# Backward sweep of a state-space scan: two products a chunk made by ScalarE, in sixteen pieces each, in place of VectorE

## The chip, the cores and the metric

The kernel runs on one core of a Trainium2 chip. A core has five engines with an instruction queue each: TensorE (matmuls, PE in the profile, with its weight loads as PEld), VectorE (DVE), ScalarE (ACT), GpSimd (POOL) and SyncE (SP). Each engine works through its queue strictly in order; semaphores tie the queues together. The metric is the device time of one launch in microseconds, as a median over runs.

## The reference, cut to what matters

The program computes two transformer-like blocks, one after the other, over 1024 tokens of width 1024. The change lies in the second block, in the backward half of a two-directional scan over chunks of 128 tokens, with 16 heads of 64 channels and a state of 128:

```python
def ssd_chunked(xs, dt, a, bm, cm, h0):
    ...
    st = jnp.einsum('bcsgn,bcsgr,bcsgrp->bcgrpn', bc, jnp.exp(acs[:, :, -1:] - acs), xdt)
    def step(s, inp):
        dec, add = inp
        return s * dec[..., None, None] + add, s
    ...
    y_off = jnp.einsum('bctgn,bcgrpn,bctgr->bctgrp', cc, s_in, jnp.exp(acs))
    return (y_diag + y_off).reshape(b, l, h, p), s_final

def bidir_ssd(xs, dt, a_log, bm, cm, h0_f, h0_b):
    ...
    y_f, s_f = ssd_chunked(xs, dt[:, :, 0], a[0], bm, cm, h0_f)
    y_b, s_b = ssd_chunked(rev(xs), rev(dt[:, :, 1]), a[1], rev(bm), rev(cm), h0_b)
    return y_f + rev(y_b), s_f, s_b
```

For a chunk, the sweep reads the state as it stands (`y_off`), then decays the state by a factor per head and adds what the chunk brings (`st`, a product of the chunk's keys with its values, the values weighed by a factor for each token and head). To the chunk's output comes also each token's own value times a factor for that token and head (the diagonal and the skip term `d_skip * xs`). Two of these are plain multiplications of a chunk's values, 128 tokens by 16 heads by 64 channels, by a number for each token and head: the own share, and the weighed values. In the kernel tokens lie on the partitions, so for one head such a number is one column of 128, and the head's values are 128x64.

In the same stretch the box means over the 16 by 64 token grid (`pool_mixer`) are made, and projections of the layer's input.

## The kernel before

`phase5` holds the scan. Its first loop is the backward sweep: eight passes, i from 0 to 7, over the chunks c = 7 - i. After it comes the forward sweep, and after that the rest of the block. All that follows is laid out engine by engine in written order; semaphores are the only ties.

One pass i, engine by engine, in queue order:

- **TensorE**: `off(0, c)`, four matmuls of the state with the chunk (L2473), once the state of pass i-1 is there; then `add_state`, four matmuls with the weighed values `xw` (L2459), once `xw_ready` says they are there; then one or two projection tiles of 48 matmuls each (`gemm`; lines L230, L232, L234). Pass 0 has one tile, passes 1, 2, 3 and 6 have two (u and z), passes 4, 5 and 7 one. The u tile goes to a pair of PSUM banks that must have been read out since the last u tile.
- **VectorE**: own share into `y_even` (L2747, after the previous `y_even` has landed in memory, `y_back`); the state's share of the output (L2749, after `off`); their sum (L2751, which signals `y_ready`); the state's decay and update (`sum_state`, L2699 and L2700, which frees the way for the next `off`); the next pass's weighed values `xw` (`weigh`, L2696); then `pool_tile(i)` (L2726 several times, L2732, L2733), the box means of the u tile, which waits until ScalarE has copied that tile out of PSUM (`pair_free`). It is 10 instructions in passes 0 and 1, 8 in 2 and 3, 6 in 4 and 5, 4 in 6 and 7. The last signals `pooled`.
- **ScalarE**: waits for `y_ready` and issues the store of `y_even` (L2617); copies the u tile out of PSUM (L2621) once it is made; in passes 0, 1, 2, 3 and 6 a Silu of a z tile and its store (L2608, L2610); waits for `pooled` and issues the store of the box means (L2593); after passes 1, 3 and 5 issues a load of the divisors (`load_area`, L2589). After pass 0 it also makes 16 scaled copies of 128x128 for the forward sweep (`make_moving(0, j)`, L2600), which nobody needs before that sweep.
- **GpSimd**: splits each weight tile into a high and a low part (L221, L223), two tiles ahead.
- **SyncE**: streams the weight tiles in.

Of the kernel before, what the change touches and what calls it, by code (L numbers as in the profile page):

```python
# [11 lines left out]
ACT = mybir.ActivationFunctionType  # L12
# [5 lines left out]
NC = SEQ // P  # L18
# [26 lines left out]
CC = CTX // P  # L45
TOK2 = CTX + SEQ
SSM_HEADS = 16
HDIM = 64
# [89 lines left out]
def bc(ap, dim, n):  # L138

    ap = ap.unsqueeze(dim)  # L140
    shape = list(ap.shape)
    shape[dim] = n
    return ap.broadcast_to(shape)
# [895 lines left out]
def signals(nc, ctx, stage, names):  # L1039

    return {n: ctx.enter_context(nc.semaphore(f"{stage}_{n}")) for n in names.split()}
# [1318 lines left out]
def phase5(nc, k, d, v):  # L2360
# [4 lines left out]
    with ExitStack() as ctx:  # L2365
        def sb(n, shape, dt=F32):
            return ctx.enter_context(nc.sbuf_tensor(n, shape, dt))

        state, y_even, xw = (sb(n, [P, SEQ]) for n in ("state5", "y5", "xw5"))
# [18 lines left out]
        ctx_values = [xw, y_even, big[:, 2, :], xw]  # L2388
        stage = k.ada_w
        s = signals(nc, ctx, "p5", "chain xw_ready moving_ready d_done chosen e_ready w_ready cb_done cb_ready off_done fore_ready "  # L2390
                                   "st_done state_ready diag_done y_ready y_back y_out0 y_out1 u_in0 u_in1 u_in2 u_in3 z_out d_out "
                                   "dhi dlo x_done x_free0 x_free1 cleared area_in pooled")
        x_free = [s["x_free0"], s["x_free1"]]
        y_out, u_in = [s["y_out0"], s["y_out1"]], [s[f"u_in{t}"] for t in range(SPLIT_EARLY)]
# [5 lines left out]
        BWD_JOBS = 2  # L2400
        after = v.consts[:, SC_FORE:SC_FORE + P].bitcast(I32)

        back = 2 * CC
        fwd = back + BWD_JOBS * NC

        def u_tile(i):
            return XBC_END + i + sum(c < i for c in Z_CHUNKS)
# [8 lines left out]
        def heads(ap):  # L2416
            return ap.rearrange("p (h n) -> p h n", h=SSM_HEADS)

        def values(c):
            return heads(v.tok[:, c, VAL:VAL + D_MODEL])  # L2420

        def per_head(buf, c, r, n=HDIM):

            return bc(buf[:, c, SSM_HEADS * r:SSM_HEADS * (r + 1)], 2, n)
# [162 lines left out]
        def _(act):  # L2587
            def load_area(g):
                act.dma_start(big[:, 3, :], d.pool_area[g, :, :]).then_inc(s["area_in"], 16)  # L2589

            def rows_out(i, t):
                act.wait_ge(s["pooled"], i + 1)
                act.dma_start(d.u_scr[t, :, :].rearrange("p (r c) -> p r c", r=ROWS), pooled).then_inc(s["d_out"], 16)  # L2593

            def make_moving(i, j):

                if i:
                    act.wait_ge(s["d_done"], QUADS * (i - 1) + j + 1)
                for h in range(j * QUAD, (j + 1) * QUAD):
                    ins = act.activation(moving[:, h, :], v.x_rows[:, i * P:(i + 1) * P], ACT.Copy,  # L2600
                                         scale=v.consts[:, SC_HEAD + h:SC_HEAD + h + 1])
                ins.then_inc(s["moving_ready"], 1)

            def z_out(i, q):
                n = z_tile(i)
                act.wait_ge(k.tile_done, n + 1)
                act.wait_ge(s["z_out"], 16 * i)
                act.activation(stage[:, :], pair[q], ACT.Silu).then_inc(k.pair_free[n % 2], 1)  # L2608
                act.wait_ge(k.pair_free[n % 2], n // 2 + 1)
                act.dma_start(d.z_scr[i, :, :], stage[:, :]).then_inc(s["z_out"], 16)  # L2610

            load_area(KT // 2 - 1)
            act.wait_ge(s["cleared"], 2)
            for i in range(NC):
                c, t = NC - 1 - i, KT - 1 - i
                act.wait_ge(s["y_ready"], i + 1)
                act.dma_start(d.y_tok[c, :, :], y_even[:, :]).then_inc(s["y_back"], 16)  # L2617
                n = u_tile(i)
                act.wait_ge(k.tile_done, n + 1)
                act.wait_ge(s["pooled"], i)  # L2620
                act.activation(u_mid, pair[n % 2].rearrange("p (r c) -> p r c", r=ROWS), ACT.Copy)\  # L2621
                   .then_inc(k.pair_free[n % 2], 1)
                if i in Z_CHUNKS:
                    z_out(Z_CHUNKS.index(i), 1)
                rows_out(i, t)
                if t % 2 == 0 and t:
                    load_area(t // 2 - 1)
                if i == 0:
                    for j in range(QUADS):
                        make_moving(0, j)  # L2630
# [59 lines left out]
        def _(dve):  # L2690
            ch = Chain(dve, s["chain"])
            tt = dve.tensor_tensor

            def weigh(c, r, out=xw[:, :]):

                tt(heads(out), values(c), per_head(v.w_st, c, r), ALU.mult).then_inc(s["xw_ready"], 1)  # L2696

            def sum_state(c, r, q):
                ch.link(tt(heads(state[:, :]), heads(state[:, :]), per_head(v.e_tot, c, r), ALU.mult))  # L2699
                tt(state[:, :], state[:, :], Xf[q], ALU.add).then_inc(x_free[q], 1)  # L2700
# [42 lines left out]
            weigh(NC - 1, 1)  # L2743
            for i in range(NC):
                c = NC - 1 - i
                dve.wait_ge(s["y_back"], 16 * i)
                ch.link(tt(heads(y_even[:, :]), values(c), bc(v.own[:, c, :], 2, HDIM), ALU.mult))  # L2747
                dve.wait_ge(s["x_done"], back + BWD_JOBS * i + 1)
                tt(heads(back_tmp), heads(Xf[0]), per_head(v.e_acs, c, 1), ALU.mult).then_inc(x_free[0], 1)  # L2749
                dve.wait_ge(x_free[0], back // 2 + i + 1)  # L2750
                tt(y_even[:, :], y_even[:, :], back_tmp, ALU.add).then_inc(s["y_ready"], 1)  # L2751
                if c:
                    dve.wait_ge(s["x_done"], back + BWD_JOBS * i + 2)
                    sum_state(c, 1, 1)
                    if c > 1:
                        weigh(c - 1, 1)
                    else:
                        weigh(0, 0)
                else:
                    dve.tensor_copy(state[:, :].rearrange("p (a n) -> p a n", a=4), state_f).then_inc(s["state_ready"], 1)  # L2760
                pool_tile(i)
# [464 lines left out]
```

## Time and profile before

| | us |
|---|---|
| Median of 3 runs | 2821.09 (2818.49 to 2828.03) |
| The profiled execution's own time | 2826.55 |
| Its span | 2824.8 |
| TensorE busy | 2659.1 (94%) |
| VectorE busy | 1638.1 (58%) |
| ScalarE busy | 609.5 (22%) |
| GpSimd busy | 995.2 (35%) |

The span is what the profiler recorded of one execution; its own time lies 1.75 us above the span. TensorE's share is near full over the whole program, so a stretch matters to the end as far as it makes TensorE stand still or run at the lower clock. The backward sweep lies at about 1544 to 1708 us of the span.

### The profile page before, as it was taken

How to read it: one execution, taken by the hardware profiler on the slowest of the kernel's cores; microseconds unless marked ns; L12 is line 12 of the kernel's file. 1: busy time of each engine (PE TensorE's matmuls, PEld its weight loads, DVE VectorE, ACT ScalarE, POOL GpSimd, SP SyncE). 2: the span in 40 equal slices, each digit the busy share in tenths (PEclk: the TensorE clock that was granted, in tenths of full speed). 3: DMA queues.
4: the chain of work that ended last, by engine and by line, in shares of the span. 5: the costliest groups of instructions: out<-in, count | busy, mean ns of one | idle time of the engine just before them, and what ended most of it. 6: DMA issues, size and time to landing. Idle time of an engine off the chain costs nothing. (4 is left out here: it accounts for less than half of the span.)

```text
span 2824.8 us, 32083 instructions
## 1 busy us (share of the span) xinstructions
PE 2659.1 (94%) x12350; PEld 2143.5 (76%) x12350; DVE 1638.1 (58%) x2219; ACT 609.5 (22%) x884; POOL 995.2 (35%) x523
## 2 busy tenths in 40 slices
PE   8889999999999999987888999889989999999997
PEld 5778777778888888866776766678767888888885
DVE  6887555756556665676846995653375222222248
ACT  4222242311110011133232104532131110001111
POOL 2122125554333343541212331113645333333353
PEclk9999999999999999998999999989999999999998
DMA  4111142222322332231001332351332111111123
GB/s 138 40 52 44 52 142 82 97 82 97 97 90 89 104 97 94 94 103 64 31 30 38 104 112 75 79 197 45 112 97 83 52 52 45 52 45 52 45 75 105
DMA packets 87332, 224.68 MB, mean 80 GB/s; under 512 B 27392, under 2 KB 30592, under 8 KB 87232
## 3 DMA queue, kind: packets, MB, share of 16 engines
q1 hardware_dynamic: 51232, 168.61, 18.0%
q10 hardware_dynamic: 34848, 50.50, 5.7%
q0 software_dynamic: 1152, 4.19, 0.9%
q8 instruction: 68, 1.11, 0.2%
q14 instruction: 32, 0.26, 0.0%
HBM read 193.79 MB, written 28.31 MB: 79 GB/s over the span
## 5 line engine op out<-in xcount | busy, mean ns | idle before, releaser
L221 POOL CAST w_hi<-w_raw 128x1024 fp32r<-128x1024 f32 x254 | 289.4, 1139 | 1691.1 <-PE ps L234 1672.0
L230 PE MATMUL ps<-a_hi,w_hi 128*128 128x512 f32 x2080 | 698.5, 404 | 51.2 <-PEq L3028 14.6
L223 POOL TENSOR_TENSOR w_lo<-w_raw,w_hi 128x1024 fp32r<-128x1024 f32 x254 | 695.7, 2739 | 20.3
L232 PE MATMUL ps<-a_lo,w_hi 128*128 128x512 f32 x2080 | 680.2, 395 | 0.0
L234 PE MATMUL ps<-a_hi,w_lo 128*128 128x512 f32 x2080 | 679.1, 394 | 0.0
L230 PEld LDWEIGHTS ps<-a_hi,w_hi 128*128 128x128 f32 x2080 | 391.2, 192 | 157.7 <-issue 68.6
L234 PEld LDWEIGHTS ps<-a_hi,w_lo 128*128 128x128 f32 x2080 | 396.7, 191 | 85.2
L232 PEld LDWEIGHTS ps<-a_lo,w_hi 128*128 128x128 f32 x2080 | 397.5, 191 | 83.9
L232 PE MATMUL ps<-g_b,w_hi 128*128 128x512 f32 x1216 | 412.1, 390 | 0.0
L230 PE MATMUL ps<-g_b,w_hi 128*128 128x512 f32 x1088 | 363.8, 392 | 11.5 <-DVE g_b L1812 11.5
L234 PE MATMUL ps<-g_b,w_lo 128*128 128x512 f32 x1088 | 361.5, 389 | 0.0
L232 PEld LDWEIGHTS ps<-g_b,w_hi 128*128 128x128 f32 x1216 | 229.1, 188 | 46.8
L230 PEld LDWEIGHTS ps<-g_b,w_hi 128*128 128x128 f32 x1088 | 204.4, 188 | 62.2 <-DVE g_b L1812 15.3
L234 PEld LDWEIGHTS ps<-g_b,w_lo 128*128 128x128 f32 x1088 | 204.5, 188 | 42.9
L1770 ACT ACTIVATE tmp_b<-ps 128x1024 f32<-128x1024 f32 x48 | 49.4, 1029 | 849.2 <-PE ps L234 849.2
L1892 DVE TENSOR_TENSOR tmp_b<-tmp_b 128x1024 f32<-128x1024 f32 x48 | 58.8, 1225 | 298.8 <-ACT tmp_b L1770 298.8
L1905 DVE TENSOR_TENSOR mix_b<-mix_b,ps 128x1024 f32<-128x1024 f32 x48 | 58.6, 1220 | 235.2 <-PE ps L234 235.2
L1894 DVE TENSOR_TENSOR g_b<-tmp_b,g_b 128x1024 fp32r<-128x1024 f32 x48 | 106.4, 2217 | 54.2 <-ACT g_b L1774 54.2
L1164 DVE TENSOR_TENSOR acc_b<-acc_b,tmp_b 128x512 f32<-128x512 f32 x56 | 77.0, 1375 | 22.8 <-ACT tmp_b L1123 19.7
L2287 DVE SCALAR_TENSOR_TENSOR cv<-raw,vecs,cv 128x1284 f32<-128x1284 f32 (+1 forms) x48 | 80.5, 1676 | 5.3 <-DVE cv L2285 0.6
L1884 DVE SCALAR_TENSOR_TENSOR ada_sum_b<-ada_w,c_silu,ada_sum_b 128x128 f32<-128x128 f32 x252 | 74.7, 345 | 3.0
L1884 DVE SCALAR_TENSOR_TENSOR ada_sum_b<-ada_w_b,c_silu,ada_sum_b 128x128 f32<-128x128 f32 x252 | 74.6, 343 | 3.0
(476 smaller groups left out, 2641.2 us busy)
## 6 DMA issues: line engine op xcount, KB each, us to landing
w_raw<-in_wstream SPq DMA_DIRECT2D x254, 512.0 KB, 3.5
ada_w<-in_ada_w ACTq DMA_DIRECT2D x25, 512.0 KB, 3.5
ada_w_b<-in_ada_w ACTq DMA_DIRECT2D x25, 512.0 KB, 3.4
x_res_b<-in_xT SPq DMA_DIRECT2D x2, 2048.0 KB, 11.4
x_block<-x_res_b SPq DMA_DIRECT2D x16, 256.0 KB, 3.1
y_by_token<-y ACTq DMA_DIRECT2D x8, 512.0 KB, 3.3
z_rows<-ada_w ACTq DMA_DIRECT2D x8, 512.0 KB, 2.6
u_rows<-pad ACTq DMA_DIRECT2D x8, 512.0 KB, 4.3
```

The costliest lines, as they stand in the source:

```text
L221: pool.tensor_copy(k.w_hi[:, s, :], k.w_raw[:, s, :]).then_inc(k.w_high, 1)
L223: pool.tensor_tensor(k.w_lo[:, s, :], k.w_raw[:, s, :], k.w_hi[:, s, :].bitcast(F32), ALU.subtract).then_inc(k.w_split, 1)
L230: pe.matmul(o, w_hi, a_hi[:, c], start=first, stop=False)
L232: pe.matmul(o, w_hi, a_lo[:, c], start=False, stop=False)
L234: ins = pe.matmul(o, w_lo, a_hi[:, c], start=False, stop=last)
L1164: dve.tensor_tensor(w.acc[:, cols], w.acc[:, cols], w.tmp[:, t % 2, cols], ALU.add).then_inc(self.added, 1)
L1770: act.activation(w.tmp[:, t % 2, :], pair[t % 2], ACT.Relu).then_inc(k.pair_free[t % 2], 1)
L1884: ins = dve.scalar_tensor_tensor(out=sums, in0=weights, scalar=k.c_silu[:, kt, c:c + 1], in1=sums, op0=ALU.mult, op1=ALU.add)
L1892: tt(w.tmp[:, t % 2, :], w.tmp[:, t % 2, :], w.tmp[:, t % 2, :], ALU.mult).then_inc(s["square"], 1)
L1894: tt(w.g_lo[:, t, :], w.tmp[:, t % 2, :], w.g_hi[:, t, :].bitcast(F32), ALU.subtract)\
L1905: tt(w.mix[:, 2 * t, :], w.mix[:, 2 * t, :], pair[q], ALU.add).then_inc(k.pair_free[q], 1)
L2287: ins = stt(out=out, in0=raw[:, m:m + cols], scalar=tap(m), in1=out, op0=ALU.mult, op1=ALU.add)
```

## The change

VectorE no longer makes the own share (L2747) or the weighed values of the next pass (L2696) inside the loop; the first `weigh`, ahead of the loop, stays. ScalarE makes both, as 16 activations each of 128x64, one for each head, whose scale is a column of 128 numbers. Line numbers below are those of the kernel after. A new semaphore `y_own` tells VectorE that the own share is there; VectorE waits for it ahead of the sum.

```diff
+            def own_values(i):
+                if i:
+                    act.wait_ge(s["y_back"], 16 * i)
+                else:
+                    act.wait_ge(s["x_done"], CC)
+                for h in range(SSM_HEADS):
+                    ins = act.activation(heads(y_even[:, :])[:, h, :], values(NC - 1 - i)[:, h, :], ACT.Copy,
+                                         scale=v.own[:, NC - 1 - i, h:h + 1])
+                ins.then_inc(s["y_own"], 1)
+
+            def weigh_next(i):
+                c, r = (NC - 2 - i, 1) if i < NC - 2 else (0, 0)
+                act.wait_ge(s["x_done"], back + BWD_JOBS * i + 2)
+                for h in range(SSM_HEADS):
+                    ins = act.activation(heads(xw[:, :])[:, h, :], values(c)[:, h, :], ACT.Copy,
+                                         scale=v.w_st[:, c, SSM_HEADS * r + h:SSM_HEADS * r + h + 1])
+                ins.then_inc(s["xw_ready"], 1)
+
             load_area(KT // 2 - 1)
+            own_values(0)
             act.wait_ge(s["cleared"], 2)
             for i in range(NC):
                 c, t = NC - 1 - i, KT - 1 - i
                 act.wait_ge(s["y_ready"], i + 1)
                 act.dma_start(d.y_tok[c, :, :], y_even[:, :]).then_inc(s["y_back"], 16)
+                if c:
+                    weigh_next(i)
                 n = u_tile(i)
...
                 rows_out(i, t)
                 if t % 2 == 0 and t:
                     load_area(t // 2 - 1)
+                if i + 1 < NC:
+                    own_values(i + 1)
                 if i == 0:
                     for j in range(QUADS):
                         make_moving(0, j)
...
             for i in range(NC):
                 c = NC - 1 - i
-                dve.wait_ge(s["y_back"], 16 * i)
-                ch.link(tt(heads(y_even[:, :]), values(c), bc(v.own[:, c, :], 2, HDIM), ALU.mult))
                 dve.wait_ge(s["x_done"], back + BWD_JOBS * i + 1)
                 tt(heads(back_tmp), heads(Xf[0]), per_head(v.e_acs, c, 1), ALU.mult).then_inc(x_free[0], 1)
                 dve.wait_ge(x_free[0], back // 2 + i + 1)
+                dve.wait_ge(s["y_own"], i + 1)
                 tt(y_even[:, :], y_even[:, :], back_tmp, ALU.add).then_inc(s["y_ready"], 1)
                 if c:
                     dve.wait_ge(s["x_done"], back + BWD_JOBS * i + 2)
                     sum_state(c, 1, 1)
-                    if c > 1:
-                        weigh(c - 1, 1)
-                    else:
-                        weigh(0, 0)
```

ScalarE's queue before, from the z store of pass 1 to pass 4 (L2617 stores y, L2621 copies the u tile, L2593 stores the box means, L2589 loads divisors):

```order
L2610 DMA z_rows<-ada_w 128x1024
L2593 DMA u_rows<-pad 2048x1x64
L2589 DMA big<-in_pool_area 128x1024
L2617 DMA y_by_token<-y 128x1024
L2621 ACTIVATE big<-ps 128x1024
```

and the same place now:

```order
L2610 DMA z_rows<-ada_w 128x1024
L2593 DMA u_rows<-pad 2048x1x64
L2589 DMA big<-in_pool_area 128x1024
L2618 ACTIVATE y<-tok,own_weight 128x64 x16
L2636 DMA y_by_token<-y 128x1024
L2626 ACTIVATE xw<-tok,w_st 128x64 x16
L2642 ACTIVATE big<-ps 128x1024
```

The own share stands behind the store of the box means and the load of the divisors; the weighed values stand between the store of y and the copy of the u tile.

ScalarE's queue now, between pass 0 and pass 1, where the 128x128 copies for the forward sweep lie:

```order
L2593 DMA u_rows<-pad 2048x1x64
L2618 ACTIVATE y<-tok,own_weight 128x64 x16
L2600 ACTIVATE moving<-x_rows,scan_consts 128x128 x16
L2636 DMA y_by_token<-y 128x1024
L2626 ACTIVATE xw<-tok,w_st 128x64 x16
L2642 ACTIVATE big<-ps 128x1024
```

Before, only the first and the last three kinds stood there, without the two rows of 128x64; now the store of y, the weighed values and the copy of the u tile all have the 16 copies of 128x128 in front of them, and these have the own share in front of them.

VectorE's queue before, from the end of pass 1's box means into pass 2's:

```order
L2732 TENSOR_TENSOR pad<-tok,big 128x16x64
L2733 TENSOR_TENSOR pad<-pad,big 128x16x64
L2747 TENSOR_TENSOR y<-tok,own_weight 128x1024
L2749 TENSOR_TENSOR big<-ps,e_acs 128x1024
L2751 TENSOR_TENSOR y<-y,big 128x1024
L2699 TENSOR_TENSOR state<-state,e_tot 128x1024
L2700 TENSOR_TENSOR state<-state,ps 128x1024
L2696 TENSOR_TENSOR xw<-tok,w_st 128x1024
L2726 TENSOR_TENSOR tok<-big 128x1408
```

and now:

```order
L2755 TENSOR_TENSOR pad<-tok,big 128x16x64
L2756 TENSOR_TENSOR pad<-pad,big 128x16x64
L2770 TENSOR_TENSOR big<-ps,e_acs 128x1024
L2773 TENSOR_TENSOR y<-y,big 128x1024
L2722 TENSOR_TENSOR state<-state,e_tot 128x1024
L2723 TENSOR_TENSOR state<-state,ps 128x1024
L2749 TENSOR_TENSOR tok<-big 128x1408
```

Two of the six instructions between the box means of one pass and the next are gone (line numbers moved by 19 to 23). TensorE's, GpSimd's and SyncE's queues keep their order.

## Rows read from the trace of the kernel before

**Rows 1.** Two stretches: length, busy us (PE, PEld, DVE, ACT, POOL), clock, DMA share, GB/s:

```profile
1544.30:1649.20 104.90, 104.54 (x424) 79.60 (x424) 103.28 (x67) 13.15 (x25) 33.41 (x15) 1.00 0.34 109
...
1663.80:1673.20 9.40, 5.46 (x8) 2.38 (x8) 9.30 (x7) 1.02 (x1) 4.53 (x2) 0.64 0.39 125
```

**Rows 2.** TensorE in order of time: start, length, instruction, [idle before <-releaser]:

```profile
1609.20 1.88 PE L2473 MATMUL ps<-state,bcT 128*128 128x512 f32 x4
...
1634.41 1.88 PE L2473 MATMUL ps<-state,bcT 128*128 128x512 f32 x4
...
1649.24 1.96 PE L2473 MATMUL ps<-state,bcT 128*128 128x512 f32 x4 [0.34 <-DVE state L2700]
...
1652.35 1.02 PE L230 MATMUL ps<-a_hi,w_hi 128*128 128x512 f32 x2
...
1667.78 3.75 PE L2473 MATMUL ps<-state,bcT 128*128 128x512 f32 x4 [3.94 <-DVE state L2700]
...
1673.46 1.03 PE L230 MATMUL ps<-a_hi,w_hi 128*128 128x512 f32 x2
...
1695.67 1.88 PE L2473 MATMUL ps<-state,bcT 128*128 128x512 f32 x4
```

**Rows 3.** VectorE in order of time, pass 4:

```profile
1641.82 1.23 DVE L2733 TENSOR_TENSOR pad<-pad,big 128x1024 f32<-128x1024 f32 x1
1642.96 1.22 DVE L2747 TENSOR_TENSOR y<-tok,own_weight 128x1024 f32<-128x1024 f32 x1
1644.22 1.23 DVE L2749 TENSOR_TENSOR big<-ps,e_acs 128x1024 f32<-128x1024 f32 x1
1645.48 1.23 DVE L2751 TENSOR_TENSOR y<-y,big 128x1024 f32<-128x1024 f32 x1
1646.62 1.22 DVE L2699 TENSOR_TENSOR state<-state,e_tot 128x1024 f32<-128x1024 f32 x1
1647.87 1.22 DVE L2700 TENSOR_TENSOR state<-state,ps 128x1024 f32<-128x1024 f32 x1
1649.01 1.22 DVE L2696 TENSOR_TENSOR xw<-tok,w_st 128x1024 f32<-128x1024 f32 x1
1650.15 2.19 DVE L2726 TENSOR_TENSOR tok<-big 128x1152 f32<-128x1152 f32 x1
```

**Rows 4.** ScalarE in order of time, the same stretch:

```profile
1643.08 0.52 ACTq L2593 DMA_DIRECT2D u_rows<-pad  x1
1643.63 1.25 ACTq L2589 DMA_DIRECT2D big<-in_pool_area  x1
1646.74 0.33 ACTq L2617 DMA_DIRECT2D y_by_token<-y  x1
1648.94 1.02 ACT L2621 ACTIVATE big<-ps 128x1024 f32<-128x1024 f32 x1 [13.30 <-PE ps L234]
```

**Rows 5.** ScalarE, a run of 128x128 copies scaled by a column:

```profile
1571.45 3.33 ACT L2600 ACTIVATE moving<-x_rows,scan_consts 128x128 fp32r<-128x128 f32 x11 [11.45 <-DVE pad L2733]
```

**Rows 6.** Groups of ScalarE's instructions by shape: busy us, mean ns of one:

```profile
L2600 ACT ACTIVATE moving<-x_rows,scan_consts 128x128 fp32r<-128x128 f32 x128 | 40.3, 391 | 12.3 <-DVE pad L2733 11.5 <-ACT ada_w L2608 0.8
...
L578 ACT ACTIVATE cs<-ang 128x32 f32<-128x32 f32 x4 | 0.9, 213 | 0.0
```

**Rows 7.** VectorE in order of time, passes 2, 3, 5 and 6:

```profile
1604.59 1.22 DVE L2700 TENSOR_TENSOR state<-state,ps 128x1024 f32<-128x1024 f32 x1
...
1626.17 1.22 DVE L2700 TENSOR_TENSOR state<-state,ps 128x1024 f32<-128x1024 f32 x1
...
1664.32 2.06 DVE L2699 TENSOR_TENSOR state<-state,e_tot 128x1024 f32<-128x1024 f32 x1
1666.41 1.22 DVE L2700 TENSOR_TENSOR state<-state,ps 128x1024 f32<-128x1024 f32 x1
...
1669.59 1.34 DVE L2726 TENSOR_TENSOR tok<-big 128x1152 f32<-128x1152 f32 x1
...
1682.09 1.22 DVE L2700 TENSOR_TENSOR state<-state,ps 128x1024 f32<-128x1024 f32 x1
```

More of the change, by code:

```diff
@@ L2390, in phase5 @@
         s = signals(nc, ctx, "p5", "chain xw_ready moving_ready d_done chosen e_ready w_ready cb_done cb_ready off_done fore_ready "
-                                   "st_done state_ready diag_done y_ready y_back y_out0 y_out1 u_in0 u_in1 u_in2 u_in3 z_out d_out "
+                                   "st_done state_ready diag_done y_ready y_own y_back y_out0 y_out1 u_in0 u_in1 u_in2 u_in3 z_out d_out "
                                    "dhi dlo x_done x_free0 x_free1 cleared area_in pooled")
```

## The prediction

> **What bounds the kernel now.** I read the busy table first: TensorE is near full over the whole program, so what counts is where it stands still. Then the windows of the backward sweep [rows 1]. From 1544.3 to 1649.2 TensorE is busy 104.5 of 104.9 us and VectorE 103.3 of 104.9: two engines full side by side, while ScalarE works 13 us. Then TensorE's own order of time [rows 2]: ahead of pass 5 it waits 0.34 us and ahead of pass 6 3.94 us, both for VectorE's state update (L2700). In the window of that second wait the granted clock is 0.64 on average, that is, part of it at 1.2 instead of 2.4 GHz. What this costs: `off` starts at 1667.78 and the next tile at 1673.46, 5.68 us on; one pass earlier, at the full clock, it was 1649.24 to 1652.35, 3.11 us. So 2.57 us of slow clock after the wait.
>
> VectorE's order of time for one pass [rows 3] shows no gap: box means end at 1643.05 (1641.82 + 1.23), own share, the state's share, their sum, two state instructions, weighed values, and the next box means at 1650.15. So up to pass 6 the sweep has two chains of nearly the same length, TensorE's tiles and VectorE's work, and TensorE's lead over the state shrinks until VectorE decides. The state is ready at 1605.81 for an `off` at 1609.20, at 1627.39 for one at 1634.41, at 1649.09 for 1649.24, at 1667.63 for 1667.78, and at 1683.31 for 1695.67 [rows 2, 3, 7].
>
> **What the change removes.** From VectorE 8 own shares and 7 weighed values at 1.22 us [rows 3]: 18.3 us. If that were all, it would shorten VectorE's chain by 1.22 or 2.44 us in every pass.
>
> **What it adds.** 15 sets of 16 scaled copies of 128x64 on ScalarE. No row has this form. The nearest is the run of 128x128 copies with the same kind of scale: 11 in 3.33 us, one of them 391 ns [rows 5, 6]. So one starts (3.33 - 0.39) / 10 = 0.294 us after the last. For 64 columns fewer I take off 64 times the price of a column, (1.02 - 0.213) us / (1024 - 32) = 0.81 ns [rows 4, 6], so 0.052: 0.242 us apart, the last one 0.34 long. A set is 15 x 0.242 + 0.34 = 3.97 us, 3.3 times the 1.22 us it replaces. Bounds: upwards no overlap at all and no gain from the smaller shape, 16 x 0.391 = 6.3 us; downwards the 128x32 row with a fixed scale, 0.213 long, less the same overlap of 0.097, plus 32 columns: 0.142 apart, 2.4 us a set. I take 3.95, since the nearest row has the same operation, the same scale operand and the same spacing.
>
> The Trainium skill has a price for this form, in "ScalarE: Activation LUTs", section "What ACT_TABLE_LOAD costs": 186 ns plus 0.833 ns a column with fixed operands, 93 ns more for each operand that is a column, and about 93 ns of overlap back to back. By that alone a set would be 15 x 0.239 + 0.33 = 3.9 us; no row here shows 64 columns. The same page's "Rules for kernel authors" says to put multiplications on VectorE, which is faster per element. Here the trace does not bear out the reason, for a 128x1024 copy takes ScalarE 1.02 us [rows 4] and the product takes VectorE 1.22 us [rows 3]; by price per element alone a set would be 1.0 us and the change would win. What speaks against it is the fixed part, paid 16 times.
>
> **Which of it is hidden.** ScalarE has time enough in total: 15 x 3.95 = 59 us beside 13 us of work in 105 us. But both sets stand where VectorE waits.
>
> *Own share.* In ScalarE's queue it comes after the store of the box means, and that waits for the end of the box means. So it starts not a moment before VectorE itself could have made it. Pass 4 [rows 3, 4]: box means end 1643.05, the issue of their store 1643.08 to 1643.60, the load of the divisors 1643.63 to 1644.88, then 16 copies until about 1648.9. The sum started at 1645.48; now it starts 3.4 us later. After passes without a load of divisors the copies end at 1647.6: 2.1 us later. Passes 2, 4 and 6 are of the first kind, 1, 3, 5 and 7 of the second. Behind the waiting sum on VectorE stand the state update, for which TensorE waits, and the box means. Pass 0 loses nothing, as its own share is made ahead of the loop.
>
> *Weighed values.* They follow the store of y and precede the copy of the u tile, for which the box means wait. Before, that copy (1.02 us) lay beside VectorE's state update. In pass 4 the sum ends at 1646.71, the store is issued until 1647.07, the copies last until 1651.0, the u copy until 1652.05: the box means start 1.9 us later than at 1650.15. In pass 5 VectorE's state update (2.06 instead of 1.22) and weighing were slower, 5.2 us from 1664.4 to 1669.59 [rows 7]; against 5.35 now that is +0.1. I use 1.9 for even passes and 0.1 for odd ones. The weighed values themselves are in time for TensorE nearly everywhere.
>
> *The 16 copies of 128x128.* They now stand between own share and store of y of pass 1: 16 x 0.294 + 0.1 = 4.8 us, of which VectorE's sum covers 1.3. Pass 1's box means start another 3.5 us later. Before, they held up nobody.
>
> **The sum.** VectorE's delay, added up (b = start of the box means, s = end of the state update): b0 1.9; s1 +2.1 = 4.0; b1 +3.6 = 7.6; s2 +3.4 = 11.0; b2 12.9; s3 15.0; b3 15.1; s4 18.5; b4 20.4; s5 22.5; b5 22.6; s6 26.0. TensorE [rows 2, 7]:
> - Pass 3: state at 1605.81 + 11.0 = 1616.8 against 1609.20. A wait of 7.6, then 2.6 of slow clock as after the wait above: 10.2 late.
> - Pass 4: TensorE at 1644.6, state at 1642.4. No wait.
> - Pass 5: TensorE free at 1649.24 - 0.34 + 10.2 = 1659.1, state at 1649.09 + 18.5 = 1667.6. Waits 8.5; 18.5 late, with slow clock 21.1.
> - Pass 6: TensorE free at 1667.78 - 3.94 + 21.1 = 1684.9, state at 1667.63 + 22.5 = 1690.1. Waits 5.2; 22.5 late. The slow clock here is in the old time too.
> - Pass 7: TensorE at 1695.67 + 22.5 = 1718.2, state at 1709.3. No wait.
>
> So the sweep ends 22.5 us later. I see nothing behind it that gives this back: the forward sweep starts from TensorE's last tile and VectorE's last box means, both shifted. The slow clock doesn't enter, since the last wait is set by VectorE and ScalarE. Against its own time, 2826.55, this makes 2849; that execution lies 5.5 us above the median, and against the median it is 2821.1 + 22.5 = 2843.6. VectorE's slow instructions (as 2.06 in rows 7) may in part fall into its new waits, so I round down: **2843 us**.
>
> **Rivals.**
> - *The copies are much cheaper.* At the lower bound of 2.4 us a set: ten sets lie on the chain up to s5, so 10 x 1.55 = 15.5 less, +7, 2828. Against it: the same operation's measured spacing. A little over +8.5 us is where this kernel's measurement can tell a change (0.3%).
> - *TensorE's lead swallows the delay.* Its lead is 3.4 us at pass 3 and 7.0 at pass 4 but nothing at passes 5 and 6, so the delay would have to stop growing after pass 2, as if the own share and the u copy were really hidden: no change, 2821. Against it stand the queue places above.
> - *Faster: VectorE is relieved and ScalarE keeps up.* The mechanism is VectorE's chain at pass 6: the waits of 0.34 and 3.94 and the slow clock of 2.57 go, 6.9 us, 2814. It decides if a set costs under about 22.5 / 10 = 2.25 us less than taken, that is 1.7 us, or 0.1 us a copy. For it: ScalarE idle 92 of 105 us. Against it: below even the fixed-scale row.
> - *Dearer: no overlap.* 6.3 us a set, ten times 2.35 more: +46, 2867. For it: two operands in memory at 64 columns might space differently. Against it: the run of 11.
>
> **How the numbers follow.** Forecast, +15 to +30: 0.83. Dearer, +30 to +46: 0.07. Cheaper copies, +7 to +15: 0.05, a good third of it within 0.3%. Lead swallows it: 0.02. Faster: 0.03. That gives faster 0.03, same 0.04, slower 0.93. For the range I let a set cost 3.5 to 4.7 us (+18 to +30), add 4 us of scatter of the medians and take in part of the cheap and the dear case: 2829 to 2856.
>
> **What would show it.** In the profile after: (1) a set of 16 copies spans 3.9 to 4.0 us; if it is far off, the term of ten sets is off by ten times that. (2) VectorE idles ahead of each sum (L2773), released by ScalarE, 2.1 us or 3.4 us in turn plus the 1.2 us of the own share it no longer makes, and ahead of the first box mean of a pass, released by the u copy, 3 us in even passes, most in pass 1. (3) TensorE waits for the state (L2723) ahead of passes 3, 5 and 6, some 8, 8 and 5 us, with a lower clock behind each. (4) The last `off` starts near 1718 instead of 1695.67. It would be wrong if VectorE's waits were there but TensorE's were not, or if the time behind the sweep shrank.

## The result, and the profile after

The changed kernel takes 2836.19 us (2832.17 to 2841.39, 6 runs) against 2821.01 us (2818.49 to 2828.03, 6 runs): ratio 1.0046, 95% interval 1.0033 to 1.0059, or 9.3 to 16.6 us more. It is slower, as forecast; the forecast of 2843 was 7 us too high. The span of the profiled execution grew from 2824.8 to 2839.6 us.

ScalarE in order of time, pass 4 of the kernel after (start, length, instruction, count), which answers to [rows 4]:

```profile
1653.74 0.52 ACTq L2593 DMA_DIRECT2D u_rows<-pad  x1
1654.29 1.25 ACTq L2589 DMA_DIRECT2D big<-in_pool_area  x1
1655.59 3.93 ACT L2618 ACTIVATE y<-tok,own_weight 128x64 f32<-128x64 f32 x16 [11.26 <-issue]
1662.31 0.33 ACTq L2636 DMA_DIRECT2D y_by_token<-y  x1
1662.69 3.93 ACT L2626 ACTIVATE xw<-tok,w_st 128x64 f32<-128x64 f32 x16 [3.17 <-DVE y L2773]
1666.52 1.00 ACT L2642 ACTIVATE big<-ps 128x1024 f32<-128x1024 f32 x1
```

VectorE in the same pass, which answers to [rows 3]:

```profile
1652.48 1.23 DVE L2756 TENSOR_TENSOR pad<-pad,big 128x1024 f32<-128x1024 f32 x1
1653.62 1.22 DVE L2770 TENSOR_TENSOR big<-ps,e_acs 128x1024 f32<-128x1024 f32 x1
1659.62 2.66 DVE L2773 TENSOR_TENSOR y<-y,big 128x1024 f32<-128x1024 f32 x1 [4.78 <-ACT y L2618]
1662.21 1.21 DVE L2722 TENSOR_TENSOR state<-state,e_tot 128x1024 f32<-128x1024 f32 x1
1663.45 1.22 DVE L2723 TENSOR_TENSOR state<-state,ps 128x1024 f32<-128x1024 f32 x1
1667.56 1.36 DVE L2749 TENSOR_TENSOR tok<-big 128x1152 f32<-128x1152 f32 x1 [2.88 <-ACT big L2642]
```

A set of 16 copies takes 3.93 us. The first begins only when the box means are over and their store and the load are issued; VectorE stands 4.78 us for it. The second stands between the store of y and the copy of the u tile; VectorE stands 2.88 us for that copy. Over the sweep, VectorE's waits as the view of waits adds them up (engine line <- releaser: us in total, times, longest):

```profile
DVE y L2773 <- ACT y L2618: 25.4, 6, 5.3
DVE tok L2749 <- ACT big L2642: 18.0, 6, 5.7
DVE pad L2749 <- ACT big L2642: 2.9, 1, 2.9
```

TensorE in order of time, the `off` of passes 3 to 7, which answers to [rows 2]:

```profile
1615.29 3.75 PE L2473 MATMUL ps<-state,bcT 128*128 128x512 f32 x4 [7.21 <-DVE state L2723]
...
1643.12 1.88 PE L2473 MATMUL ps<-state,bcT 128*128 128x512 f32 x4
...
1664.82 3.59 PE L2473 MATMUL ps<-state,bcT 128*128 128x512 f32 x4 [7.21 <-DVE state L2723]
...
1683.65 1.95 PE L2473 MATMUL ps<-state,bcT 128*128 128x512 f32 x4 [2.62 <-DVE state L2723]
...
1709.14 1.88 PE L2473 MATMUL ps<-state,bcT 128*128 128x512 f32 x4
```

It waits 7.21 us ahead of pass 3, nothing ahead of pass 4, 7.21 ahead of pass 5 and 2.62 ahead of pass 6. The four matmuls after the two long waits take 3.75 and 3.59 us, after the short one 1.95.

From here on "the sweep" is the time from the first `off` to the last: 151.31 us before (1544.36 to 1695.67) and 166.06 after (1543.08 to 1709.14), 14.75 more. The span grew by 14.8; what lies ahead of the sweep and behind it differs by a few us either way. It is a steadier measure than the time of a run, which differs by up to 16 us between executions of the kernel before. The windows of the sweep, with the columns of [rows 1], before:

```profile
1544.36:1695.67 151.31, 147.03 (x584) 110.62 (x585) 146.04 (x96) 15.96 (x27) 47.61 (x20) 0.98 0.33 105
```

and after:

```profile
1543.08:1709.14 166.06, 149.01 (x584) 111.01 (x585) 117.14 (x78) 65.94 (x235) 41.08 (x20) 0.95 0.30 95
```

VectorE is busy 28.9 us less, with 18 instructions fewer: 15 products that left it, and three box means of pass 6 that now lie behind the last `off` (3.30, 1.22 and 1.22 us before). So the two windows do not hold the same work. From the first `off` to the end of the state update of pass 5 they do, save for 11 products (a twelfth has just begun). First before and then after:

```profile
1544.36:1667.63 123.27, 119.14 (x480) 90.02 (x480) 121.38 (x79) 14.94 (x26) 42.29 (x18) 0.99 0.33 107
1543.08:1683.51 140.43, 123.53 (x480) 91.45 (x480) 102.16 (x67) 54.31 (x194) 35.59 (x18) 0.94 0.30 94
```

VectorE is busy 19.2 us less here, and 11 products at 1.22 are 13.4. The rest, nearly 6 us, is time by which instructions were longer before, the products that left among them. GpSimd is busy 6.7 us less with the same 18 instructions.

### The profile page after: what moved, and what is told of

It reads as the page before. It is cut to its first block and busy times, and to the rows that moved or that the text cites. A ratio compares the mean times of both kernels' runs of the same rounds, so it can differ in the third digit from the quotient of the medians.

```text
span 2839.6 us, 32308 instructions
## 1 busy us (share of the span) xinstructions
PE 2667.1 (94%) x12350; PEld 2148.8 (76%) x12350; DVE 1614.2 (57%) x2204; ACT 667.6 (24%) x1124; POOL 989.9 (35%) x523
## 5 line engine op out<-in xcount | busy, mean ns | idle before, releaser
L234 PE MATMUL ps<-a_hi,w_lo 128*128 128x512 f32 x2080 | 678.9, 394 | 0.0
L234 PEld LDWEIGHTS ps<-a_hi,w_lo 128*128 128x128 f32 x2080 | 396.9, 191 | 85.3
L234 PE MATMUL ps<-g_b,w_lo 128*128 128x512 f32 x1088 | 362.0, 390 | 0.0
L234 PEld LDWEIGHTS ps<-g_b,w_lo 128*128 128x128 f32 x1088 | 204.8, 188 | 43.0
```

Source lines behind the costliest of these rows:

```text
L234: ins = pe.matmul(o, w_lo, a_hi[:, c], start=False, stop=last)
```

## The experiments

The gain or loss of a kernel against before is given twice below: by the sweep in its profile, and, where it was run several times, by the ratio of its runs to those of the kernel before on the same chip.

### Own shares only

Against the changed kernel, the weighed values go back to VectorE:

```diff
-                if c:
-                    weigh_next(i)
...
                     sum_state(c, 1, 1)
+                    if c > 1:
+                        weigh(c - 1, 1)
+                    else:
+                        weigh(0, 0)
```

> Own shares on ScalarE, weighed values back on VectorE. Theory (place in the queue): the copies begin only after the box means and their store, and VectorE's sum waits for them, 2.1 us later than before in odd passes, 3.4 us in even ones. Up to the state update of pass 5 that is 2.1 + 3.4 + 2.1 + 3.4 + 2.1 = 13.1 us less what the loss of slow VectorE instructions gives back; in the kernel with both moved, 17.2 of 22.5 were seen, so some 8 to 12 us over before: 2829 to 2833. VectorE's waits ahead of the sum stay at 3.5 and 4.7 us; no wait ahead of the box means. Rival (it is the weighed values and the u copy behind them that cost): within 3 us of before, 2818 to 2824.

Measured: ratio 1.0014 (1.0001 to 1.0027), median 2828.45; sweep 154.95, 3.6 more than before. VectorE's waits ahead of the sum are there, 3.5 to 3.6 and 4.7 to 4.8 us in turn. TensorE waits 7.70 us ahead of pass 5 and not at all ahead of pass 6:

```profile
1655.22 3.75 PE L2473 MATMUL ps<-state,bcT 128*128 128x512 f32 x4 [7.70 <-DVE state L2721]
...
1672.52 1.88 PE L2473 MATMUL ps<-state,bcT 128*128 128x512 f32 x4
```

The expectation of 8 to 12 us was too high: the state of pass 5 came 6.0 us later than before (each from its own first `off`), and with the wait ahead of pass 6 went the slow clock behind it, 2.6 us.

### Weighed values only

The own share goes back to VectorE:

```diff
-            own_values(0)
...
-                if i + 1 < NC:
-                    own_values(i + 1)
...
+                dve.wait_ge(s["y_back"], 16 * i)
+                ch.link(tt(heads(y_even[:, :]), values(c), bc(v.own[:, c, :], 2, HDIM), ALU.mult))
...
-                dve.wait_ge(s["y_own"], i + 1)
```

> Weighed values on ScalarE, own shares back on VectorE. Theory (place in the queue): the u copy and with it the box means come 1.9 us later in even passes, 0.1 in odd ones, and 3.5 to 4 more in pass 1 if the 16 copies of 128x128 still stand ahead, which they now do without the own share ahead of them (about 1.7 to 3.5): some 6 to 8 us up to pass 5, of which VectorE's lost slow instructions give back a part: +2 to +6, 2823 to 2827. Rival (weighed values are the costly part): +10 or more, 2831. If both parts simply add up, this run and the one with own shares only exceed the kernel before by 15 together.

Measured: sweep 155.43, 4.1 more than before, as the theory had it. But the ratio is 1.0039 (1.0026 to 1.0052), median 2835.14, some 11 us more, as the rival had it. In the profile 3.1 us of the rest lie between the first exponents and the loads of the next block (142.49 against 139.44, see the repeated profiles below), some 2.4 behind those loads, where two profiles of one kernel (the one with both products early, below) differ by 3.3. What the sweep loses by this part is seen in its one profile; what the runs lose beyond it stays open.

The two parts alone lose 3.6 and 4.1 in the sweep, together 14.75. At pass 5 the delays still nearly add up: `off` comes 7.6 and 8.4 us later by either part alone, 16.9 by both. The difference comes behind it. Before, TensorE waited 3.94 us ahead of pass 6 and then ran 2.6 us longer at the lower clock. By either part alone the long wait, with the low clock behind it, lies ahead of pass 5 (7.70 and 6.94 us), none is left ahead of pass 6, and part of the delay is won back there. By both together TensorE still waits 2.62 us ahead of pass 6.

### Both products early

The same copies by ScalarE in other places of its queue (`pass_out` is what stood at the end of a pass: `rows_out`, `load_area` and, once, `make_moving`):

```diff
             for i in range(NC):
                 c, t = NC - 1 - i, KT - 1 - i
+                if c:
+                    weigh_next(i)
+                if i:
+                    pass_out(i - 1)
                 act.wait_ge(s["y_ready"], i + 1)
                 act.dma_start(d.y_tok[c, :, :], y_even[:, :]).then_inc(s["y_back"], 16)
-                if c:
-                    weigh_next(i)
...
                 act.activation(u_mid, pair[n % 2].rearrange("p (r c) -> p r c", r=ROWS), ACT.Copy)\
                    .then_inc(k.pair_free[n % 2], 1)
+                if i + 1 < NC:
+                    own_values(i + 1)
                 if i in Z_CHUNKS:
...
-                rows_out(i, t)
...
-                if i + 1 < NC:
-                    own_values(i + 1)
```

> Both products on ScalarE as 16 copies each, but in other places of its queue: the weighed values at the start of a pass (as soon as TensorE has read the old ones), the own share of the next pass right after the copy of the u tile, the store of the box means after the weighed values. Theory (place in the queue, not the price of the copies): ScalarE has room, VectorE's chain is shorter by 1.2 to 2.4 us a pass, and TensorE's waits of 0.34 and 3.94 us with 2.6 us of slow clock go: -5 to -7, 2814 to 2816. Rival (16 small copies cost too much wherever they stand, or ScalarE's traffic slows VectorE): 2821 or more, with VectorE instructions longer than 1.22 us while ScalarE copies.

Measured: sweep 145.69, 5.6 less than before and 20.4 less than the changed kernel. VectorE's timeline shows neither the own share nor the weighed values as a wait; pass 3:

```profile
1614.59 1.22 DVE L2777 TENSOR_TENSOR big<-ps,e_acs 128x1024 f32<-128x1024 f32 x1
1615.84 1.23 DVE L2780 TENSOR_TENSOR y<-y,big 128x1024 f32<-128x1024 f32 x1
1616.98 1.22 DVE L2729 TENSOR_TENSOR state<-state,e_tot 128x1024 f32<-128x1024 f32 x1
1618.24 1.22 DVE L2730 TENSOR_TENSOR state<-state,ps 128x1024 f32<-128x1024 f32 x1
1623.20 1.63 DVE L2756 TENSOR_TENSOR tok<-big 128x1408 f32<-128x1408 f32 x1 [3.74 <-ACT big L2654]
```

and TensorE waits once, 1.47 us, ahead of pass 6; its row and the window of the sweep:

```profile
1663.12 1.96 PE L2473 MATMUL ps<-state,bcT 128*128 128x512 f32 x4 [1.47 <-DVE state L2730]
...
1542.75:1688.44 145.69, 144.22 (x584) 109.76 (x585) 127.76 (x81) 70.58 (x251) 46.13 (x20) 1.00 0.35 109
```

The wait of 3.74 us for the u copy is of another kind: TensorE has not made that tile any sooner. The theory holds for the sweep: the same 15 sets at the same price (3.93 us where one runs through) lose 14.75 us in one place of the queue and gain 5.6 in another. But the ratio is 0.9998 (0.9986 to 1.0010): in the whole kernel there is no gain that the runs can tell.

### One piece in place of sixteen

Each set is one copy of 128x1024 with one head's column for all heads, so both products are not the reference's:

```diff
-                for h in range(SSM_HEADS):
-                    ins = act.activation(heads(y_even[:, :])[:, h, :], values(NC - 1 - i)[:, h, :], ACT.Copy,
-                                         scale=v.own[:, NC - 1 - i, h:h + 1])
+                ins = act.activation(heads(y_even[:, :]), values(NC - 1 - i), ACT.Copy,
+                                     scale=v.own[:, NC - 1 - i, 0:1])
```

and likewise for the weighed values.

> As the changed kernel, same queue places, but each set is one copy of 128x1024 with one head's column for all heads (so the own share and the weighed values are not those of the reference). Theory: a set takes 1.05 instead of 3.93 us; ten sets on the chain give 29 us more than the delay there was, so VectorE's chain is no longer than before in any pass but the first: between -6 and +1 against before, 2815 to 2822. Rival (the waits between engines cost, not the length of the sets): at least a third of the loss stays, 2826 or more.

Measured: a set takes 1.15 us (1.05 was expected), in the queue places of the changed kernel:

```profile
1645.06 1.15 ACT L2617 ACTIVATE y<-tok,own_weight 128x1024 f32<-128x1024 f32 x1 [8.04 <-issue]
```

The sweep is 148.02, 3.3 less than before; the ratio is 0.9992 (0.9981 to 1.0002). So the loss needs both: the late place and 16 pieces. With short sets the late place costs 2.3 us against the early one (148.02 against 145.69) and the sweep is still shorter than before. The Trainium skill's rule that multiplications go to VectorE ("ScalarE: Activation LUTs", section "Rules for kernel authors") gives as its reason VectorE's speed per element in bf16. The copies here are f32, where one of 128x1024 with a column as its scale takes 1.15 us against VectorE's 1.22; here what speaks against ScalarE is what each of 16 instructions costs beside its elements.

### The 128x128 copies moved ahead of the loop

```diff
             own_values(0)
+            for j in range(QUADS):
+                make_moving(0, j)
...
-                if i == 0:
-                    for j in range(QUADS):
-                        make_moving(0, j)
```

> The changed kernel with only the 16 copies of 128x128 for the forward sweep moved, from behind the own share of pass 1 to ahead of the loop, where ScalarE idles. I measure the sweep by the time from the first off (state with chunk) to the last: 151.3 us before, 166.1 in the changed kernel. Theory (ScalarE's place in the queue decides): VectorE's box means of pass 1 start 3.5 us sooner and every state update after it 3.5 us less whatever slow VectorE instructions shift: 162 to 163.5; the whole run some 3 us under the changed kernel, 2833. Rival (those copies were hidden): 166.

Measured: sweep 166.06, to the hundredth that of the changed kernel; ratio 1.0062 (1.0045 to 1.0079). The rival's number, but not by the rival's reason, for VectorE's wait in pass 1 did shrink from 5.74 to 3.21 us. In this kernel the box means of pass 1 start 2.5 us sooner after the first `off` (39.59 against 42.12) and then take longer. GpSimd (two rows) and VectorE (two rows) in pass 1 of this run:

```profile
1581.05 2.72 POOL L221 CAST w_hi<-w_raw 128x1024 fp32r<-128x1024 f32 x1 [7.38 <-PE ps L234]
1583.86 4.06 POOL L223 TENSOR_TENSOR w_lo<-w_raw,w_hi 128x1024 fp32r<-128x1024 f32 x1
```

```profile
1580.72 2.16 DVE L2748 TENSOR_TENSOR tok<-big 128x1920 f32<-128x1920 f32 x1 [3.21 <-ACT big L2644]
1582.92 6.61 DVE L2748 TENSOR_TENSOR tok<-tok 128x1792 f32<-128x1792 f32 x2
```

The same two instructions took 3.82 us in the changed kernel. And in pass 2 of both kernels the sum ends 69.66 us after the first `off`, though it started 0.4 us sooner here, because it ends 1.07 us after GpSimd's split in both. The changed kernel:

```profile
1609.33 2.34 POOL L223 TENSOR_TENSOR w_lo<-w_raw,w_hi 128x1024 fp32r<-128x1024 f32 x1
```

```profile
1610.96 1.78 DVE L2773 TENSOR_TENSOR y<-y,big 128x1024 f32<-128x1024 f32 x1 [5.30 <-ACT y L2618]
```

The split ends at 1611.67, the sum at 1612.74. Here the split (1607.38 for 2.34) ends at 1609.72 and the sum (1608.65 for 2.14) at 1610.79. TensorE's tile releases the split (`<-PE ps L234` above), so the split pins what VectorE does beside it. This is read from the rows; no run moved the copies with the splits thinned.

### Thin splits

In both kernels GpSimd splits 8 of 1024 columns of each weight tile during this scan, so the projections of the second block are not the reference's:

```diff
-            stream_split(pool, k, XBC_END + 2, UZ_END)
+            for n in range(XBC_END + 2, UZ_END):
...
+                pool.tensor_copy(k.w_hi[:, s_, 0:8], k.w_raw[:, s_, 0:8]).then_inc(k.w_high, 1)
+                pool.wait_ge(k.w_high, n + 1)
+                pool.tensor_tensor(k.w_lo[:, s_, 0:8], k.w_raw[:, s_, 0:8], k.w_hi[:, s_, 0:8].bitcast(F32),
+                                   ALU.subtract).then_inc(k.w_split, 1)
```

The changed kernel so thinned:

> The changed kernel, with GpSimd splitting only 8 of 1024 columns of each weight tile in this scan (the projections of the second block are then not those of the reference); TensorE and ScalarE do the same work. Theory (VectorE's long instructions are those beside GpSimd's splits): all VectorE instructions of 128x1024 in the sweep take 1.2 us, none 2 or 3; first to last off about 154 us instead of 166.1. Rival (their length comes from something else, as ScalarE's or DMA traffic): 2 to 3.4 us ones stay, 166.

The kernel before so thinned:

> The kernel before, with GpSimd splitting only 8 of 1024 columns of each weight tile in this scan (projections of the second block are not the reference's). Theory: VectorE's chain drops well under TensorE's, no wait for the state in passes 5 and 6, no slow clock: first to last off 144.4 us (151.3 less 6.9). With the run of the changed kernel so thinned at 154, the change costs 9.5 us here against 14.8 with the splits. Rival (VectorE's long instructions do not come from GpSimd): 151.

Measured: sweep 155.81 in the changed kernel (1539.27 to 1695.08) and 146.53 in the kernel before (1542.82 to 1689.35). Every VectorE product or sum of 128x1024 in both takes 1.22 to 1.26 us. Over the same work, from the first `off` to the end of the state update of pass 5, the changed kernel and then the kernel before:

```profile
1539.27:1669.45 130.18, 123.29 (x480) 91.55 (x480) 88.46 (x67) 54.74 (x194) 10.06 (x18) 0.96 0.32 101
1542.82:1663.88 121.06, 120.55 (x480) 90.69 (x480) 101.25 (x79) 14.54 (x26) 11.88 (x18) 0.99 0.34 109
```

VectorE's busy time there falls from 121.4 to 101.3 us in the kernel before and from 102.2 to 88.5 in the changed one. So the splits held VectorE up 20.1 us before and 13.7 after: the change gave back 6.4 us of it. In both profiles a spell of slow clock in pass 0 took 1.7 us (the second `off` starts 16.1 us after the first, in place of 14.4); without it the sweeps are 154.1 and 144.8, where 154 and 144.4 were expected (a wait of 0.65 us ahead of pass 6 stayed in the second). With the splits thinned, the change costs 9.3 us in place of 14.75.

### Early, with the 128x128 copies ahead

The kernel with both products early, and `make_moving(0, j)` ahead of the loop as above.

> Both products early in ScalarE's queue, as in the run with both early (first to last off 145.7 us), and the 16 copies of 128x128 ahead of the loop. Theory: the last wait of 1.47 us ahead of pass 6 goes, 144.3 us, TensorE never waits in the sweep; the whole run 6 to 7 us under before if the time behind the sweep does not change, 2815 to 2817. Rival (what is gained in the sweep is lost behind it, as the medians of the run with both early suggest: sweep 5.6 shorter, median the same): within 3 us of before, with the time from the first exponents to the loads of the next block longer than 139.4 us by what was gained.

Measured: sweep 145.65, against 145.69 without the move; the wait ahead of pass 6 stays, 1.45 us. Ratio 1.0001 (0.9989 to 1.0013), median 2822.83. The theory's 144.3 us did not come, and the median is the rival's. Its account holds for a part: the first exponents (TensorE's first matmul of the forward sweep that makes them) are 159.56 us after the first `off`, but from there to the loads of the next block it is 142.36 us, where before has 139.44. So 2.9 of the 5.7 us gained are lost there. The other 2.8 are 0.1% of the whole, less than the runs can tell.

### Repeated profiles

> The kernel before once more, for a second profile. Two readings of why the sweep that is 5.6 us shorter leaves the median where it was. Theory A (the sweep's length is fixed, what lies behind it scatters with where the clock falls): first to last off again 151.3 within 0.3, the forward sweep (first exponents to the loads of the next block) anywhere in 136 to 143 us against 139.4 in the first profile. Theory B (a kernel has its own forward sweep): 139.4 again.

> The kernel with both products early once more, for a second profile. Theory A: first to last off 145.7 again, forward sweep elsewhere than 141.8, by 1 us or more. Theory B (the shorter sweep always costs some in the forward sweep, through another place of the slow clock): 141.8 again, with the clock at 0.83 some 60 to 70 us after the first exponents as in the first profile, so 2.4 of the 5.6 us are given back there each time.

> The kernel before a third time, for a third profile: as the second, it tells whether the 139.4 us of the forward sweep are the kernel's own (theory B, 139.4 again) or one draw of several (theory A).

| Profile | First to last off | First exponents to loads of the next block | First off to those loads |
|---|---|---|---|
| Before, first | 151.31 | 139.44 | 304.7 |
| Before, second | 151.21 | 139.52 | 304.6 |
| Before, third | 153.10 | 139.86 | 306.9 |
| Both early, first | 145.69 | 141.81 | 301.4 |
| Both early, second | 145.64 | 142.35 | 301.9 |
| Both early, copies ahead | 145.65 | 142.36 | 301.9 |
| Changed kernel | 166.06 | 137.11 | 317.7 |

The third profile of before has the spell of slow clock in pass 0, 1.7 us. The second column speaks for theory B: a kernel keeps its own forward sweep within 0.6 us, and with the products early it is some 2.5 us longer. That is three profiles against three; why a shorter sweep should have this effect is not shown. One place of it is a stretch of 10 us, 60 us after the first exponents. Both early and then before, the columns as above:

```profile
1762.36:1772.36 10.00, 8.34 (x24) 4.45 (x23) 6.53 (x6) 7.93 (x14) 5.06 (x3) 0.83 0.49 104
```

```profile
1769.59:1779.59 10.00, 8.09 (x32) 4.53 (x30) 8.13 (x8) 8.41 (x15) 5.06 (x3) 1.00 0.48 104
```

The clock there is 0.83 against 1.00 (the second profile of each has the same two values), and the forward sweep's next matmuls of keys with queries come 1.3 us later. So of 5.6 us gained in the sweep about 3 are left at the next block. The rest of the time scatters more than that: the first `off` of the three profiles of before lies at 1544.36, 1538.55 and 1547.41 us. Three us is 0.1%, at the edge of the interval of the ratio, so whether the version with both early beats the kernel before by them stays open. It beats the changed kernel by some 13 us, going by the two ratios to before (0.9998 and 1.0046).

## Why the prediction was right or wrong

**What bounds the sweep: right.** TensorE waited ahead of passes 3, 5 and 6 and not ahead of 4 and 7, as worked out.

**The price of a set: right.** 3.97 and 3.95 us were worked out from the 128x128 copies, 3.93 was measured. The estimate by the formula of the Trainium skill ("ScalarE: Activation LUTs", section "What ACT_TABLE_LOAD costs"), 3.9, agrees with the trace as well.

**Which of it is hidden: right, and shown.** VectorE's waits were forecast as 3.3 and 4.6 us in turn ahead of the sum and measured as 3.5 to 3.6 and 4.7 to 5.3. Ahead of the box means 3 us were forecast for even passes, and 2.9 came. With the same sets elsewhere in the queue the loss turns into a gain in the sweep.

**The 16 copies of 128x128: the wait was right, the term was not worth what it was put at.** It was there in pass 1 (5.74 us in place of 3.21), but taking it away gave back nothing. By the rows, GpSimd's split then held VectorE up.

**The sum: the mechanism right, the size off.** How much later VectorE's state update ended than before, by the prediction and measured, in us (s1 is that of pass 1; measured from each kernel's own first `off`, which came 1.28 us sooner after):

| | s1 | s2 | s3 | s4 | s5 | s6 |
|---|---|---|---|---|---|---|
| Predicted | 4.0 | 11.0 | 15.0 | 18.5 | 22.5 | 26.0 |
| Measured | 3.1 | 10.6 | 13.2 | 16.9 | 17.2 | 23.5 |

Up to s2 the terms hold within 1 us. The step that was mis-sized is carrying VectorE's own durations over from before. The prediction took rows with lengths of 2.06 and the like as fixed and wrote only that they "may in part fall into its new waits". They did: up to s5 VectorE lost 19.2 us of busy time where 11 products at 1.22, 13.4 us, were removed. What made them long was GpSimd's split beside them, shown by the thin splits (20.1 us before, 13.7 after). At s5 the delay is 17.2 in place of 22.5, 5.3 less. The largest piece of this, 3.7, is in pass 5: from s4 to s5 the delay was to grow by 4.0 and grew by 0.3. Three instructions on that way were long before: 2.19 us [rows 3], 2.06 us [rows 7] and the one of 3.30 us here, with GpSimd's row beside it:

```profile
1652.37 3.30 DVE L2726 TENSOR_TENSOR pad<-tok 128x1024 f32<-128x1024 f32 x1
1651.21 3.38 POOL L223 TENSOR_TENSOR w_lo<-w_raw,w_hi 128x1024 fp32r<-128x1024 f32 x1
```

After, the same three take 1.36, 1.23 and 1.22, which is 3.7 us less. GpSimd had made its split around the end of VectorE's wait for the own share, beside the sum of 2.66 us, and then stood idle:

```profile
1668.95 1.23 DVE L2749 TENSOR_TENSOR pad<-tok 128x1024 f32<-128x1024 f32 x1
1658.86 2.34 POOL L223 TENSOR_TENSOR w_lo<-w_raw,w_hi 128x1024 fp32r<-128x1024 f32 x1
1681.17 1.98 POOL L221 CAST w_hi<-w_raw 128x1024 fp32r<-128x1024 f32 x1 [19.97 <-PE ps L234]
```

The second piece is the slow clock behind the wait ahead of pass 6. The prediction says that it "is in the old time too" and so cancels. But the state came 5.3 us sooner than forecast, the wait was 2.62 us in place of 5.2, and TensorE came out of it at the full clock (1.95 us in place of 3.75 in [rows 2]). Together: 22.5 - 5.3 - 2.4 = 14.8, and 14.75 was measured. This piece of 2.4 us was not bound to come: in the run with one piece a wait of 2.07 us at the same place had the lower clock behind it.

These two pieces are the third of the forecast 22.5 us that did not come in the sweep. The range, +8 to +35 us, was wide enough to hold them.

**Nothing behind the sweep gives it back: near enough.** The forward sweep took 137.1 in place of 139.4 us in the one profile of the changed kernel; the stages behind it took 3.1 us more. For one stretch of the version with both early such a difference is shown to be one of slow clock; for these two it is not shown.

**The rivals.** Cheaper and dearer copies are out by the measured 3.93. TensorE's lead swallowed the delay at pass 3 only when one product was moved, all but 0.1 us of it with own shares only and all but 1.5 with weighed values only, and even then pass 5 started 7.6 and 8.4 us later. The faster rival, VectorE relieved, is what happens with the copies placed early, but in the sweep alone: the runs show no gain.

## What to carry to other kernels

Work moved to an idle engine that takes longer for it helps only if it stands in that engine's queue ahead of the moment the old engine would have made it itself. Ask for each piece what the instruction in front of it waits for; here both stood behind something that VectorE had just finished, at 3.93 us in place of 1.22. Many small pieces with a scale each should be priced by the spacing of such pieces (0.24 us here), not by their elements. And durations on two engines that hold each other up are not constants: when one gets gaps, part of the loss comes back.

## What the runs showed of the hardware

**VectorE and GpSimd hold each other up, instruction by instruction.** It depends on the operands. The state's two instructions in the sweep of the changed kernel (durations in ns, shortest, median, longest):

```profile
L2722 DVE TENSOR_TENSOR state<-state,e_tot x7: 1211/1218/3418, 1547.5 to 1703.1; 128x1024 f32<-128x1024 f32 x7
L2723 DVE TENSOR_TENSOR state<-state,ps x7: 1220/1220/1222, 1548.7 to 1704.3; 128x1024 f32<-128x1024 f32 x7
```

The one that reads two tensors from SBUF grew to 3.42 us beside a split; the one that reads one of the two from PSUM never grew, though GpSimd worked beside it too, as at 1682.29 (GpSimd's cast of 1681.17 to 1683.15). The Trainium skill says in "SBUF — State Buffer", section "Who interferes with whom", that a VectorE instruction with two SBUF inputs contends with a GpSimd instruction that reads SBUF, for a shared port pair that one of them holds as an exclusive lock. The rows agree as far as they go: the sum of pass 2 ended 1.07 us after the split in two kernels, and the state's instruction of 3.42 us 1.09 after the split that ended at 1637.01. GpSimd pays as well: a split of 2.34 us took 4.06 in the run with the 128x128 copies ahead.

**The clock was low behind every long pause of TensorE in the sweep and behind no short one, but in between the length of the pause does not settle it.** The four matmuls of `off` take 1.88 us at the full clock. After the ten pauses of 3.94 to 7.70 us they took 3.59 to 3.75, after the nine of 0.23 to 1.83 us 1.95 or 1.96. In between both are seen: 1.95 after 2.62 us in the changed kernel and after 2.59 in the one with the 128x128 copies ahead, but 3.03 after 2.07 us ahead of pass 6 in the run with one piece:

```profile
1666.75:1671.75 5.00, 5.00 (x9) 2.18 (x9) 4.93 (x3) 0.00 (x0) 1.92 (x1) 0.66 0.33 103
```

The clock in these 5 us is 0.66, that is, part of it at the lower of the two levels. And the pause of 2.73 us ahead of pass 0 was followed by 1.95 or 1.96 in ten profiles, and by 2.83, 3.15 and 3.36 in three, the spells of slow clock in pass 0 named above.
